# Local attention: who writes the masks and when the scores are issued; sparse units: a head's queries and a gate copy moved

## The reference

```
scores = einsum(q, k) * 64 ** -0.5
scores = where(band, scores, -1e30)
probs  = softmax(concat([scores, sink]))[..., :-1]
out    = einsum(probs, v)
```

## Time and profile before

| | |
|---|---|
| median of three runs | 1989.44 us |
| the profiled execution | 1986.43 us |
| its span | 1984.6 us |
| TensorE busy in the span | 1966.2 us (99%) |
| VectorE | 1031.9 us (52%) |
| ScalarE | 806.3 us (41%) |
| GpSimd | 269.9 us (14%) |
| TensorE clock granted | 0.999 of full |

### The profile page before, as it was taken

One profiled execution on the slowest core, in us unless ns is written; L12 is line 12 of the kernel. 1 busy time (PEld: TensorE's weight loads), 2 busy tenths in 40 slices (PEclk: granted clock), 3 DMA queues, 4 the chain that ended last, 5 costly groups with the idle time before them and its releaser, 6 DMA issues.

```text
span 1984.6 us, 25302 instructions
## 1 busy us (share of the span) xinstructions
PE 1966.2 (99%) x10027; PEld 1661.6 (84%) x10027; DVE 1031.9 (52%) x1587; ACT 806.3 (41%) x1471; POOL 269.9 (14%) x280
## 2 busy tenths in 40 slices
PE   9999999999999999999999999999999999999998
PEld 7888988888888888888988788888888888888887
DVE  6766665555353222333563768877765543222333
ACT  6542543333343222333333763566663342222332
POOL 1001000000000000000003542477860000000000
PEclk9999999999999999999999999999999999999999
DMA  6331333333223333332453144211225323332332
GB/s 206 103 107 61 110 106 96 95 96 98 99 91 106 96 96 95 96 98 83 126 153 113 47 154 144 77 54 49 64 83 194 113 80 109 97 96 95 96 96 74
DMA packets 60102, 201.15 MB, mean 101 GB/s; under 512 B 8305, under 2 KB 8337, under 8 KB 59602
## 3 DMA queue, kind: packets, MB, share of 16 engines
q1 hardware_dynamic: 56082, 184.58, 29.7%
q0 software_dynamic: 3904, 14.97, 2.2%
HBM read 180.12 MB, written 8.39 MB: 95 GB/s over the span
## 4 chain that ended last, share of the span: by engine, by line
PE 91%; DVE 3%; ACT 2%; POOL 1%; issue 1%; DVEq 1%; DMA 1%; POOLq 0%; SPq 0%; ACTq 0%
PE ps L709 27%; PE ps L711 26%; PE ps L710 26%; PE ps L1240 1%; PE ps L1278 1%; PE ps L1277 1%; PE ps L1220 1%; PE ps L1221 1%; PE ps L1147 1%; POOL PU L665 1%; ACT XN L1404 1%; PE ps L892 1%; DVE XN L1932 1%; PE ps L806 1%; PE ps L870 0%
## 5 line engine op out<-in xcount | busy, mean ns | idle before, releaser
L1892 DVE TENSOR_TENSOR Wl<-raw,Wh 128x1024 fp32r<-128x1024 f32 x307 | 377.9, 1233 | 689.8 <-ACT Wh L1371 688.4
L709 PE MATMUL ps<-HTh,Wh 128*128 128x512 f32 (+1 forms) x1712 | 641.4, 375 | 2.4 <-DVE gst L2488 1.0
L711 PE MATMUL ps<-HTh,Wl 128*128 128x512 f32 (+1 forms) x1712 | 636.8, 372 | 0.0
L710 PE MATMUL ps<-HTl,Wh 128*128 128x512 f32 (+1 forms) x1712 | 636.5, 372 | 0.0
L1371 ACT CAST Wh<-raw 128x1024 fp32r<-128x1024 f32 x307 | 321.8, 1051 | 734.2 <-DMA raw<-in_w_all 734.1
L709 PEld LDWEIGHTS ps<-HTh,Wh 128*128 128x128 f32 x1712 | 322.6, 188 | 56.8 <-issue 1.9
L711 PEld LDWEIGHTS ps<-HTh,Wl 128*128 128x128 f32 x1712 | 322.4, 188 | 56.3
L710 PEld LDWEIGHTS ps<-HTl,Wh 128*128 128x128 f32 x1712 | 322.7, 188 | 53.1
L709 PE MATMUL ps<-Wh,Yh 128*128 128x512 f32 (+1 forms) x532 | 206.5, 388 | 0.0
L711 PE MATMUL ps<-Wh,Yl 128*128 128x512 f32 (+1 forms) x532 | 206.2, 388 | 0.0
L710 PE MATMUL ps<-Wl,Yh 128*128 128x512 f32 (+1 forms) x532 | 206.1, 387 | 0.0
(11 more groups left out here) (303 smaller groups left out, 2272.2 us busy)
## 6 DMA issues: line engine op xcount, KB each, us to landing
raw<-in_w_all SPq DMA_DIRECT2D x307, 512.0 KB, 3.6
swp_d<-qkd SPq DMA_DIRECT2D x64, 64.0 KB, 2.9
g_dram<-gst SPq DMA_DIRECT2D x16, 256.0 KB, 3.9
ring<-g_dram POOLq DMA_DIRECT2D x16, 256.0 KB, 3.6
X<-in_x SPq DMA_DIRECT2D x4, 512.0 KB, 5.5
swp_r<-qkr SPq DMA_DIRECT2D x16, 128.0 KB, 3.6
gpre<-in_g_pre POOLq DMA_DIRECT2D x4, 512.0 KB, 4.2
Kh<-Kh SPq DMA_DIRECT2D x16, 128.0 KB, 2.3
```

The lines of the kernel that those rows point to most:

```text
L709: tensor.matmul(dst, a_hi, b_hi, start=start, stop=False)
L710: tensor.matmul(dst, a_hi, b_lo, start=False, stop=False)
L711: return tensor.matmul(dst, a_lo, b_hi, start=False, stop=stop)
L1892: vector.tensor_tensor(Wl[:, s, :], raw[:, s, :], Wh[:, s, :], ALU.subtract).then_inc(w_lo, 1)
```

## The change

Seven edits:

- `band` becomes 512 columns wide (the two masks twice).
- For heads 0 and 1, `local_scores` writes the mask of a whole bank with one matmul (384 columns for bank 0, 512 for bank 1) ahead of the scores; the mask matmuls of line 982 go, for all heads.
- For heads 2 to 7 the masks are in the banks already. `local_exps(h)` for h = 1 to 6 ends with a drain, which raises the new counter `l_exp`, and two copies from `band` into bank 0 (384 columns) and bank 1 (512 columns). These copies free the banks, and the exponentials of these heads no longer do.
- `local_gate(h)` waits for `l_exp` for these heads.
- TensorE issues scores(h+2) behind rope_r(h+3) or vg, and no longer ahead of it.
- GpSimd runs queries(2) ahead of weigh(1).
- Gate chunk 0 is copied from bank 7 by ScalarE, behind the exponentials of the compressed scores, and not by VectorE.

```diff
-        band = sb("band", [P, 2 * P], BF16)
-        causal = band[:, P:]
+        band = sb("band", [P, 4 * P], BF16)
+        causal = band[:, P:2 * P]
...
                 weigh(0)
+                pl.wait_ge(roped, 28)
+                pl.wait_ge(full[2], FILLED["nsa"][2] + 2)
+                queries(2)
                 for s in range(32):
                     if s < 31:
                         weigh(s + 1)
                     h = s // 2 + 2
-                    if s % 2 == 0 and h < 16:
+                    if s and s % 2 == 0 and h < 16:
...
                     for b, o, p, i in LOCAL:
+                        w = P if i == 0 else 2 * P
                         if i % 2 == 0:
                             bank_free("local", b, h)
-                        w = P if i == 0 else 2 * P
+                            if h < 2:
+                                m = slice(P, 4 * P) if b == 0 else slice(0, 4 * P)
+                                tensor.matmul(ps[b][:, 0:m.stop - m.start], identb[:], band[:, m], start=True, stop=False, skip_group_check=True)
...
-                        tensor.matmul(dst, q, kah[:, kv, k], start=True, stop=False)
-                        tensor.matmul(dst, q, kal[:, kv, k], start=False, stop=False)
-                        last = tensor.matmul(dst, identb[:], band[:, 2 * P - w:], start=False, stop=True)
+                        tensor.matmul(dst, q, kah[:, kv, k], start=False, stop=False, skip_group_check=True)
+                        last = tensor.matmul(dst, q, kal[:, kv, k], start=False, stop=i % 2 == 1, skip_group_check=True)
...
                     local_turn(h)
-                    if h < 6:
-                        local_scores(h + 2)
                     if h < 5:
                         rope_r(h + 3)
...
+                    if h < 6:
+                        local_scores(h + 2)
                     local_values(h)
...
-                        if i % 2:
+                        if h in (0, 7) and i % 2:
                             last.then_inc(free[b], 1)
+                    if 1 <= h < 7:
+                        scalar.drain().then_inc(l_exp, 1)
+                        scalar.copy(ps[0][:, 0:3 * P], band[:, P:4 * P]).then_inc(free[0], 1)
+                        scalar.copy(ps[1][:], band[:]).then_inc(free[1], 1)
...
                 unit_exps(0)
                 cmp_exp(1)
+                chunk_done("nsa", 0)
+                scalar.copy(gst[0][:], ps[7][:]).then_inc(free[7], 1)
...
-                    for b in range(2):
-                        ve.wait_ge(free[b], FREED["local"][b] + h + 1)
+                    if h in (0, 7):
+                        for b in range(2):
+                            ve.wait_ge(free[b], FREED["local"][b] + h + 1)
+                    else:
+                        ve.wait_ge(l_exp, h)
...
                 unit_max(1)
-                gate_out(0)
                 cmp_weigh(1)
```

More of the change, by code:

```diff
@@ L331, in program @@
         l_prob = sem("l_prob")
+        l_exp = sem("l_exp")
         l_hi = sem("l_hi")
@@ L2163, in _ @@
             vector.tensor_copy(identb[:], masks_f[:, 2, :])
-            vector.tensor_copy(causal, masks_f[:, 0, :])
-            vector.tensor_copy(band[:, 0:P], masks_f[:, 1, :])
+            for two in range(2):
+                vector.tensor_copy(band[:, 2 * two * P:(2 * two + 1) * P], masks_f[:, 1, :])
+                vector.tensor_copy(band[:, (2 * two + 1) * P:(2 * two + 2) * P], masks_f[:, 0, :])
             vector.tensor_scalar(nsinks[:], sinks[:], -1.0, None, ALU.mult)
```

## The result

The changed kernel takes 1997.64 us (median of five runs, 1995.13 to 2000.03), the kernel before 1988.46 us beside it. The ratio is 1.0048 with a 95% interval of 1.0038 to 1.0058: 9.5 us slower (7.6 to 11.5). The forecast was 1992.2, the range ended at 1996.5. The sign of the forecast's sum was right; its size was not.

The account below looks back on a forecast made before the run. The prediction took TensorE, busy 99% of the span, as the bound. Local stage +4.3 us and sparse units -1.5 gave +2.8, on the median 1992.2 us (+0.14%), range 1986.0 to 1996.5.

Parts of the forecast that it names:

- the term of the mask: ScalarE's drain and two mask copies per head: 0.97 us, range 0.82 to 1.27, counted for heads 2 to 6.
- the step that failed: End of local stage: scores(7) fills bank 1 by 116.3, values(5) starts near 118.0, turn(6) at 119.9, 4.3 us later.
- TensorE's beat: TensorE's time per local head: 8.52 us before, 8.08 without its mask matmuls.
- Masks in the loop: VectorE and ScalarE loop per head grows from 8.27 to 9.24 us, exceeds TensorE's beat and becomes the bound.
- The last stall: TensorE, behind scores(7), waits about 2 us ahead of values(5) for max(7)'s second half and the first low part.
- The sparse part: Sparse units' start: GpSimd's 1.29 us wait goes and the gate copy comes 0.2 us earlier; 1.5 us gained.
- the loop is longer than walked: Rival, ScalarE between exponentials and weight cast: drain and copies cost 1.5 us per head, sum +5.4, 1994.8 us; chance 0.35.
- Only the last stall remains: Rival: the loop fits, TensorE loses only about 2 us between scores(7) and values(5); -2.2, 1987.2 us; chance 0.13.
- all of it pays: Rival: no new wait in the local stage and the sparse gain holds; -4.2, 1985.2 us; chance 0.08.
- The sparse part fails: Rival, sparse units: weigh(1) becomes late and the gain is lost; +4.3, 1993.7 us; chance 0.04.
- the first rival: Same as the loop is longer than walked: mask drain and copies at 1.5 us per head, 1994.8 us; chance 0.35.

Follow-up runs that it names:

- e4: Changed kernel with ScalarE's rope_out(7) copy moved ahead of the exponentials and masks of head 6; 1992.71 us, ratio 1.0023 to the kernel before.
- e5: Changed kernel with sixteen unread matmuls on TensorE ahead of the first vg part, filling its wait for rope_out(7); 1995.19 us, ratio 1.0041 to the kernel before.
- e10: Kernel before with only the sparse edits, plus one TensorE wait for gate(6) ahead of the first vg part; 1992.33 us, ratio 1.0024.
- e6: Changed kernel with ScalarE's masks written later, after the next head's ALh copies and low rows; 1992.33 us, ratio 1.0016 to the kernel before.
- e3: Changed kernel with all masks written by TensorE and no ScalarE mask copies or drain, new order kept; 1991.2 us, ratio 1.0016 to the kernel before.
- e8: Changed kernel with masks late and rope_out(6), rope_out(7) early, max(7) still ahead of low(5); 1988.27 us, ratio 1.0003 to the kernel before.
- e2: Changed kernel with the scores ahead of the rotary chunk again, ScalarE still writing the masks; 1989.25 us, ratio 1.0002 to the kernel before.
- e1: Kernel before with the sparse edits alone (queries(2) ahead of weigh(1), gate chunk 0 copied by ScalarE); 1988.18 us, ratio 0.9997.
- e7: Changed kernel with masks late, rope_out(6) and rope_out(7) early, and max(7) behind gate(6); 1984.23 us, ratio 0.9987 to the kernel before.
- e9: Like e8, but scores(7) sits between the two vg chunks, masked by TensorE, without masks(6); 1983.79 us, ratio 0.9982 to the kernel before.

## Why the prediction was wrong

The forecast for the local stage was +4.3 us, it was +12.3. Three terms make up the difference. Their sizes are estimates from the rows of the profiled execution:

- +0.9: the term of the mask. Forecast 0.97 us per head; the rows of after show 0.22 for the drain (the copy starts at 89.71; without a drain it would at about 89.49), 0.42 and 0.52, so 1.16 us. Exponentials to cast are 3.17 us against 2.01, the same 1.16. The loop then is 8.27 + 1.16 = 9.43; measured 9.41. Five heads with 0.19 more are 0.9. The Trainium skill, page "ScalarE: Activation LUTs", section "What ACT_TABLE_LOAD costs", had the copies closer than I took them: 186 ns + 0.833 ns per column less 93 ns is 0.41 and 0.52. The trace agrees. In whole it was within my range of 0.82 to 1.27.
- +3.0: **the step that failed.** "TensorE must sit through max(7)'s second half (0.94) and the first low part (0.74)" took it for given that TensorE gets to scores(7) without a wait, over the `vg` part. But `vg`'s token tile writes banks 6 and 7, and bank 7 is freed by rope_out(7) on ScalarE, whose queue has exps(6) and masks(6) ahead of that copy. I had ScalarE in "its masks until 115.6" in my own walk and looked only at what they held up for scores(7), not at what was queued behind them. By the times of that walk the copy ends near 116.2; nine matmuls of `vg` at 0.23 us and 0.9 us of scores follow, so bank 1 is full near 119.2 and not at 116.3. TensorE waited 3.47 us (to 120.01). e4 shows the wait by moving that one copy.
- +4.1: the granted clock, a term that the prediction didn't have at all. The waits of 3.47 and 1.71 us were followed by 10.2 us at 1.2 GHz. The size is what is left over (12.3 - 4.3 - 0.9 - 3.0), and the rows give it too. From the first matmul into bank 7 to the last reduction of max(7) 5.95 us pass here (120.01 to 125.96), and 3.27 in e5, where the clock was full (119.20 to 122.47). From turn(6) to the sixth matmul behind it 3.54 us pass (129.48 to 133.02), and 1.97 at turn(7) (135.52 to 137.49). That is 2.7 + 1.6 = 4.3 us. The two reductions, after and then e5:

```profile
125.96 0.69 DVE L2204 TENSOR_REDUCE lmx<-ps 128x2 f32<-128x512 f32 x1 [0.23 <-PE ps L988]
```

```profile
122.47 0.68 DVE L2208 TENSOR_REDUCE lmx<-ps 128x2 f32<-128x512 f32 x1
```

e10 gives 1.5 us for 3.4 us of lower clock, and 10.2 us at half speed lose 5.1 us at most. The Trainium skill, page "TensorE: Matmul & The Clock Gate", section "HAM oscillation — how this bites in real kernels", describes a kernel in which a wait between bursts of matmuls is paid a second time, as the next burst starts cold. The trace agrees that matmuls behind a wait run at half speed. It differs in two things: in e10 the first five matmuls behind the wait still ran at full speed, and in e4 no single wait was over 1.8 us and the clock fell all the same. I should have asked about the clock at the 2 us stall that I forecast myself.

What held:

- TensorE's beat: 8.08 us forecast, 8.06 measured. Scores without masks take 0.93 us (76.05 to 76.98).
- Masks in the loop, as the order of ScalarE says: starts of max 9.2 us apart forecast, 9.3 to 9.4 measured. TensorE waits 0.56 us ahead of each turn from head 3 on, where "about 0.8" was forecast, and about 0.2 ahead of the values of heads 2 and 3. From start to start a head loses more, 9.41 less 8.06, so 1.35 us. e6 shows that the masks' place is what holds up the loop.
- The last stall: "2 us ahead of values(5)"; it was 1.71 us, and 1.7 in e3, e4 and e8 as well, so it comes from the order of scores(7), max(7) and values(5).
- The sparse part: -1.5 us forecast, 1.50 shorter in every kernel that has it. The rule of the Trainium skill, page "SBUF — State Buffer", section "Who interferes with whom", weighed in the prediction at 0.1 us, made no visible difference.

Of the rivals, *the loop is longer than walked* comes nearest in sign but not in mechanism: it decided from 1.2 us per head, and the price was 1.16. *Only the last stall remains* and *all of it pays* fall with the loop of 9.41 us. *The sparse part fails* falls with the table. None held the missed wait or the clock. The upper end of the range, 1996.5, is also not reached by any sum that the prediction names: +5.8 - 1.5 gives 1993.7, the first rival 1994.8. So there was some room for the unseen, and too little.

What stays open: the stage of the changed kernel is from one profiled execution, the slowest of its five (2000.03 us; the others are 1995.13 to 1999.96), and the 9.5 us of the ratio (7.6 to 11.5) are under the 10.8 that 12.3 - 1.5 gives, though inside its interval. The mean granted clock of the whole execution is 0.997 or 0.998 in all five, and 0.999 or 1.000 in every execution of the kernel before. That points to a fall in each of the five, by different amounts. What it cost in the other four was not shown, so 4.1 us is the price in the profiled execution and may be less in the median.

## What to carry to other kernels

When an instruction is added to an in-order queue, list everything behind it up to the last item of the stage, and for each the bank or buffer that it frees. The engine that was never late before has no row to warn of it. Where a stall of TensorE of one or two microseconds is forecast, add a term for matmuls behind it at the lower clock: here it fell behind a wait of 1.7 us with shorter ones ahead of it (e4), and stayed full through four of up to 1.5 us (e2). And before work is moved to an idle engine, see in which of its gaps it lands: the same two copies cost 1.16 us per head between exponentials and cast, and nothing of the loop's time in the idle stretch ahead of the exponentials.

## What the runs showed of the hardware

- **The clock falls after short waits.** 3.4 us at 1.2 GHz followed one wait of 3.56 us (e10), and one of 1.7 us with seven of 0.7 or less ahead of it (e4). Four waits with 3.8 us in sum and 1.5 at most brought none (e2). 3.4 us at the lower clock cost 1.5 us in e10, the stage length less that of e1 and the wait. The other kernels with 3.4 us give 0.8 (e3), 1.1 (e4) and 1.6 (e8), less exactly, since a walk stands in each of these differences.
- **The start has two forms.** Times of one kernel lie in two groups: e7's eleven runs are 1983.7 to 1984.8 (seven) and 1986.7 to 1987.3 (four). The profiled execution of e7 is in the lower group and has the short warm-up (2.15 us for the four matmuls at 5 us, where the kernel before has 1.98); that of e9 is in the upper group of its runs (1985.8 to 1987.2 against 1983.3 to 1984.3) and has 3.78. Of the others, e3, e5, e6 and e8 have the short form (1.98 to 2.37), the changed kernel, e1, e2, e4 and e10 the long one. That is nearly 3 us, more than most effects in this case, and only the stage lengths see past it. In the long form three bf16 matmuls of 512 columns take 1.46 us where they take 0.82 in the short one, which is the difference between 0.43 and 0.23 us from start to start. So a later rise from the lower clock would explain the two forms; the profile's granted clock reads 1.00 in both between 5 and 9 us, so that stays an inference.
